# Computing the next head pair's queries and gates inside the attention of the current one

## The chip, the cores and the metric

The kernel runs on the 8 cores of one Trainium2 chip. Each core has five engines with a queue of their own, which meet only through semaphores: TensorE (PE, matmuls; PEld is its weight load), VectorE (DVE), ScalarE (ACT), GpSimd (POOL) and SyncE (SP, which only issues DMAs). An engine runs its own instructions in the order in which the program wrote them. The metric is the time of the slowest core in microseconds, median over runs; lower is better.

## The reference

One encoder layer, applied to one sequence of 8192 tokens ("p") and four of 2048 ("s"), width 2048. There are 8 heads of kind A (global attention, two key/value heads) and 8 of kind B (a neighbourhood of 8 by 16 positions plus a learned bias); both see 16 meta tokens ahead of the sequence.

```python
u = rms_norm(h, norm_w) @ w_in
qa, ka, va, za, qb, kb, vb, zb = split(u)
qa = rope(rms_norm(qa, q_norm_a)); ka = rope(rms_norm(ka, k_norm_a))
ya = softmax(qa @ ka.T * scale) @ va * silu(za)             # all tokens
qb = rms_norm(qb, q_norm_b); kb = rms_norm(kb, k_norm_b)
yb = softmax(qb @ kb.T * scale + bias, window + meta) @ vb * silu(zb)
y  = h + concat(ya, yb) @ w_out
```

## The kernel before, in words

No core talks to another. Each does four chunks of 512 query tokens: two of the long sequence (64 key tiles, `nt = 64`, chunks 0 and 1), then two of a short one (`nt = 16`, chunks 2 and 3). Keys and values of the A heads are computed once for a sequence and stay in SBUF (`KAT`, `VAE`).

**A chunk.** Nine tiles of 128 tokens are normalised and transposed into `xnTl`. Then four *head pairs* `hp` = 0 to 3 are done, each with two B heads and two A heads, and last the output projection. Of the six groups of 256 weight columns that a pair needs, four are for B (`qb`, `kb`, `vb`, `zb`), two for A: `qa` (queries) and `za` (gates, through Silu). A *projection* is 16 matmuls of 128x256 into one PSUM buffer (`proj`, L331). `qb` has 4 of them, `kb` 9, `vb` 9, `zb` 4, `qa` 4, `za` 4. The work of each pair:

- `gen_bproj(hp)`: the B projections. It begins with the bias tiles `BT`, four times two DMAs on the POOL queue (L545), then a POOL add of the mask (L548), all one behind the other. It is a generator; each `next` does one *step*: one projection, and for `qb` and `kb` also the statistics of the item before (ACT L352 to L357, POOL L361) and the last part of the item before that (`qk_final`: DVE L392, two transposes L397, copies L404). With the steps that only drain, B has 6 + 11 + 9 + 4 = 30 steps.
- `battn(hp)`: B attention, 8 items (L594 to L625), exponentials on ACT (L607 to L611). It is the reader of `BT`.
- `aphase(hp)`: first `qa` with rope (POOL L368, L376 and L382 beside L361; 4 items in 6 steps), then `za` (4 steps). Then, for each of two heads, A attention in *units* of two key tiles: scores `S` (L666, two matmuls of 128x512), one exponential over 128x1024 (L671), and `PV` (L693, 8 matmuls). That is 33 units a head for `nt = 64` and 9 for `nt = 16`, the last of each with only the 16 meta tokens. While they run, a step of `gen_bproj(hp + 1)` is called after every second unit (`nt = 64`) or after each (`nt = 16`).

**Buffers.** Outside A attention a projection takes turns between two PSUM buffers in `psA`. During A attention, `S` uses `psA`, and all projections share one buffer in `ps_m` ("single" mode): the next can start only when the last has been copied out. What is left of the generator after attention (12 steps for `nt = 16`, none for `nt = 64`) runs with two buffers again. The A queries `QTA` and gates `ZGA` exist once.

**Weights.** Two slots `ws`. `nextw()` hands out a group and issues the load of the one behind it. In chunk 0 that is a DMA on the POOL queue with a cast (L253), a multiplication of 4.4 us on DVE (L255), and a store to DRAM on SP; afterwards it is one DMA on SP. The rope tables of `qa` come through SP too (L411).

**The activation table.** Silu needs another table on ACT than Exp, Ln and Square do. Each change shows as an ACT_TABLE_LOAD in front of the instruction.

## Time and profile before

| | |
|---|---|
| median of 2 runs | 4385.31 us (4384.64 to 4385.98) |
| the profiled execution | 4396.51 us |
| its span, from the first instruction to the last | 4395.5 us (core 2, the slowest) |
| spans of the eight cores | 4344.3 to 4395.5 us |
| busy PE / PEld / ACT / DVE / POOL | 66 / 50 / 43 / 26 / 22% of the span |
| mean granted TensorE clock | 0.845 of full speed |
| ACT_TABLE_LOAD | 1283 ns each; 40 in front of L671, 34 of L523, 16 of L526 |

The span is the sum of stages with different limits, so its averages say little. The page was read for the sizes of things, the table of stretches for the stages, and the list in order of time for what each stage waits for. Full clock is 2.4 GHz; a granted share of 0.50 is 1.2 GHz.

### The profile page before, as it was taken

The numbers are of one execution on the slowest core, as the hardware profiler recorded it, in microseconds if no ns is written. First come the engines' busy times: TensorE is split into PE (matmuls) and PEld (weight loads), VectorE is DVE, ScalarE is ACT, GpSimd is POOL, SyncE is SP. The second block draws the span as 40 slices with busy tenths as digits, with TensorE's granted clock in tenths as the row PEclk, the third lists the DMA queues.
The fourth block names the chain that finished last, engine by engine and source line by source line (L and its number), as shares of the span: only waits on it lengthen the run. The fifth ranks groups of instructions, "written<-read, shape, count | busy, mean of one in ns | idle before, by whom it ended". The sixth has DMA issues, their size and how long they took to land.

```text
span 4395.5 us, 74263 instructions; the slowest of 8 cores (4344.3 to 4395.5 us)
## 1 busy us (share of the span) xinstructions
PE 2906.0 (66%) x24964; PEld 2191.3 (50%) x24964; DVE 1138.5 (26%) x2810; ACT 1902.1 (43%) x4001; POOL 959.1 (22%) x1463
## 2 busy tenths in 40 slices
PE   3777465758566734777776776666676766677677
PEld 2666343535444423554554545554554555455455
DVE  4666432222222002211111102522122113222221
ACT  3777423635444603354545561643343304333330
POOL 2555413030211001211112100513213200321310
PEclk9999687979887966988878898988888877788788
DMA  5555745242422267211112005632313352322214
GB/s 146 195 195 195 152 80 72 49 65 49 78 45 51 44 133 164 61 35 48 28 37 39 34 31 194 180 102 44 64 44 54 58 163 105 55 60 47 44 56 132
DMA packets 331472, 376.61 MB, mean 86 GB/s; under 512 B 177504, under 2 KB 299104, under 8 KB 299104
## 3 DMA queue, kind: packets, MB, share of 16 engines
q1 hardware_dynamic: 76176, 298.36, 19.8%
q0 software_dynamic: 236496, 56.72, 14.5%
q10 hardware_dynamic: 18432, 16.79, 1.1%
q8 instruction: 212, 3.47, 0.3%
q14 instruction: 156, 1.28, 0.1%
HBM read 376.09 MB, written 52.43 MB: 97 GB/s over the span
## 4 chain that ended last, share of the span: by engine, by line
PE 46%; DMA 18%; ACT 13%; issue 9%; DVE 7%; POOL 6%; ACTq 0%; DVEq 0%; SPq 0%; POOLq 0%
PE psA L331 21%; PE ps_m L331 10%; DMA BT<-rw 8%; ACT PT L671 6%; PE ps_o L693 5%; PE psA L666 4%; DMA xres<-xloc 3%; POOL BT L548 2%; DVE qtok L392 2%; DMA xf<-xloc 2%; PE psA L319 2%; DMA ws<-w_out 2%; PE ps_m L397 2%; DMA ws<-w_in 1%; POOL BT L545 1%
## 5 line engine op out<-in xcount | busy, mean ns | idle before, releaser
L331 PE MATMUL psA<-ws,xnTl 128*128 128x256 bf16 x7488 | 970.7, 295 | 13.5 <-DVE VBE L519 6.2
L671 ACT ACTIVATE PT<-psA,negc 128x1024 bf16<-128x1024 f32 x640 | 685.7, 1111 | 627.7 <-PE psA L666 625.9
L331 PEld LDWEIGHTS psA<-ws,xnTl 128*128 128x128 bf16 x7488 | 780.0, 106 | 156.4 <-issue 16.7
L361 POOL TENSOR_TENSOR wxg<-wk,gt 128x256 f32<-128x256 f32 x354 | 259.0, 733 | 2096.9 <-DVE wk L346 2082.9
L693 PEld LDWEIGHTS ps_o<-VAE,PT 128*128 128x128 bf16 (+1 forms) x5248 | 341.9, 100 | 483.1 <-issue 434.2
L693 PE MATMUL ps_o<-VAE,PT 128*128 128x129 bf16 (+1 forms) x5248 | 427.6, 226 | 229.3 <-ACT PT L671 223.8
L331 PE MATMUL ps_m<-ws,xnTl 128*128 128x256 bf16 x3840 | 518.5, 294 | 38.7 <-DVE wk L346 38.7
L397 PE MATMUL ps_m<-identb,qtok 128*128 128x128 bf16 x708 | 103.3, 230 | 632.7 <-DVE qtok L392 632.5
L304 ACT ACTIVATE xb<-xf 128x2048 bf16<-128x2048 f32 x118 | 225.4, 1910 | 524.3 <-DMA xf<-xloc 352.8
L331 PEld LDWEIGHTS ps_m<-ws,xnTl 128*128 128x128 bf16 x3840 | 392.5, 105 | 106.8 <-issue 40.4
L666 PE MATMUL psA<-QTA,KAT 128*128 128x512 bf16 x1280 | 405.3, 405 | 10.9 <-ACT ZGA L526 10.9
L352 ACT ACTIVATE wt<-wk 128x128 f32<-128x128 f32 x708 | 218.3, 308 | 432.8 <-DVE wk L346 387.6
L331 PE MATMUL psA<-ws,OT 128*128 128x256 bf16 x2048 | 284.4, 310 | 173.5 <-DVE ysb L735 170.7
L397 PEld LDWEIGHTS ps_m<-identb,qtok 128*128 128x128 bf16 x708 | 49.3, 99 | 693.8 <-issue 693.8
L331 PEld LDWEIGHTS psA<-ws,OT 128*128 128x128 bf16 x2048 | 224.3, 111 | 233.1 <-issue 182.8
L319 PE MATMUL psA<-identb,xb 128*128 128x128 bf16 x1888 | 157.6, 250 | 228.9 <-DVE xb L310 227.9
L319 PEld LDWEIGHTS psA<-identb,xb 128*128 128x128 bf16 x1888 | 136.9, 113 | 246.4 <-issue 238.6
L548 POOL TENSOR_TENSOR BT<-BT,cmb 128x1280 bf16<-128x1280 bf16 x64 | 171.7, 2683 | 400.2 <-DMA BT<-rw 392.9
L419 DVE RECIPROCAL rl<-ps_o 128x1 f32<-128x1 f32 x256 | 41.9, 164 | 686.0 <-PE ps_o L693 431.3
L376 POOL TENSOR_TENSOR wt<-wxg,rope 128x64 f32<-128x64 f32 x584 | 169.3, 322 | 174.5 <-ACT wt L352 174.5
L310 DVE TENSOR_SCALAR xb<-xf,st 128x2048 bf16<-128x2048 f32 x118 | 155.1, 1315 | 170.4 <-ACT st L308 170.1
L523 ACT ACT_TABLE_LOAD x34 | 43.6, 1283 | 293.9 <-PE psA L331 239.6
(74 smaller groups left out, 2989.6 us busy)
## 6 DMA issues: line engine op xcount, KB each, us to landing
ws<-wbf SPq DMA_DIRECT2D x98, 1024.0 KB, 5.1
xf<-xall_p SPq DMA_DIRECT2D x64, 1024.0 KB, 5.3
xf<-xloc SPq DMA_DIRECT2D x38, 1024.0 KB, 6.6
wbf<-ws SPq DMA_DIRECT2D x34, 1024.0 KB, 4.6
ws<-w_in POOLq DMA_DIRECT2D x26, 1024.0 KB, 9.2
BT<-rw POOLq DMA_DIRECT2D x128, 160.0 KB, 5.2
xres<-xloc SPq DMA_DIRECT2D x128, 128.0 KB, 4.7
y<-ysb ACTq DMA_DIRECT2D x128, 128.0 KB, 3.5
```

The lines of the kernel that those rows point to most:

```text
L304: op("act", lambda: ACTE.activation(out=xb[i][:], in_=xf[i][:], func=ACT.Square, accum_out=st[i][:, 0:1]), reads=[t_xf[i]], writes=[t_xb[i ...
L310: op("dve", lambda: DVE.tensor_scalar(out=xb[i][:], in0=xf[i][:], scalar1=st[i][:, 2:3], scalar2=None, op0=ALU.mult), reads=[t_xf[i], t_st ...
L319: op("pe", lambda c=c, hf=hf, c8=c8: PE.transpose(out=pst(hf)[:, c8, :], in_=xb[i][:, c * 128:(c + 1) * 128], identity=identb[:]), reads=[ ...
L331: op("pe", lambda c=c: PE.matmul(psu(pu), lhsT=xT_fn(c), rhs=ws[wslot][:, c, :], start=(c == 0), stop=(c == 15)), reads=txl + [t_ws[wslot] ...
L352: op("act", lambda h=h: ACTE.activation(out=wt2[k][:, h * 128:(h + 1) * 128], in_=wk[k][:, h * 128:(h + 1) * 128], func=ACT.Square, accum_ ...
L361: op("pool", lambda: POOL.tensor_tensor(out=v3(wxg[k]), in0=v3(wk[k]), in1=gb, op=ALU.mult), reads=[t_wk[k], t_gt], writes=[t_wxg[k]])
L376: op("pool", lambda hh=hh, s_=s_: POOL.tensor_tensor(out=ov[:, 2 * hh:2 * hh + 2, s_, :], in0=xv[:, 2 * hh:2 * hh + 2, 1 - s_, :], in1=sv[ ...
L397: op("pe", lambda h=h: PE.transpose(out=ps_m[:, m, h * 128:(h + 1) * 128], in_=qtok[q_][:, h * 128:(h + 1) * 128], identity=identb[:]), re ...
L548: op("pool", lambda bi=bi: POOL.tensor_tensor(out=BT[bi][:].rearrange("p h (r c) -> p (h r) c", r=10), in0=BT[bi][:].rearrange("p h (r c) ...
L666: op("pe", lambda c=c, bank=bank: PE.matmul(psA[:, bank, :], lhsT=KAT[:, g, c * 128:(c + 1) * 128], rhs=QTA[:, hl, :], start=True, stop=True),
L671: op("act", lambda: ACTE.activation(out=PT[p_][:].rearrange("p (a n) -> p a n", a=2), in_=psA[:, 2 * sp_:2 * sp_ + 2, :], func=ACT.Exp, bi ...
L693: op("pe", lambda j=j, c=c, i_=i_, kc=kc: PE.matmul(pso(j), lhsT=PT[p_][:kc, i_ * 512 + j * 128:i_ * 512 + (j + 1) * 128], rhs=VAE[:kc, c, ...
```

## The change

`QTA` and `ZGA` become pairs of buffers, indexed by `hp % 2`. The `qa` and `za` projections leave `aphase` and become a generator `gen_aproj(hp)`, which `gen_next(hp)` runs behind `gen_bproj(hp)`: 40 steps in all. `gen_next(0)` runs ahead of `battn(0)`, and `gen_next(hp + 1)` is stepped during the A attention of `hp`. The pace is no longer one step for so many units: after unit `u`, as many steps have been called as 46 times `u` over the number of units (66 or 18), rounded down. All 40 are then done after 58 of 66 units, and after 16 of 18. To make room in SBUF, the residual and output tiles `xres` and `ysb` of the output projection now share the buffers of `wxg` and `wt1`.

```diff
@@ -166,14 +166,14 @@
-        QTA = sb("QTA", [128, 2, 512], BF16); t_QTA = Tk()
-        ZGA = sb("ZGA", [128, 4, 256], BF16); t_ZGA = Tk()
+        QTAs = [sb(f"QTA{i}", [128, 2, 512], BF16) for i in range(2)]; t_QTAs = [Tk(), Tk()]
+        ZGAs = [sb(f"ZGA{i}", [128, 4, 256], BF16) for i in range(2)]; t_ZGAs = [Tk(), Tk()]
...
-        xres = [sb(f"xres{i}", [128, 256], F32) for i in range(2)]; t_xres = [Tk(), Tk()]
-        ysb = [sb(f"ysb{i}", [128, 256], F32) for i in range(2)]; t_ysb = [Tk(), Tk()]
+        xres, t_xres = wxg, t_wxg
+        ysb, t_ysb = wt1, t_wt1
@@ -523,8 +523,8 @@
-                            op("act", lambda: ACTE.activation(out=ZGA[:, it["j"], :], in_=psu(pu), func=ACT.Silu),
-                               reads=[t_pu(pu)], writes=[t_ZGA])
+                            op("act", lambda: ACTE.activation(out=it["zga"][:, it["j"], :], in_=psu(pu), func=ACT.Silu),
+                               reads=[t_pu(pu)], writes=[it["t_zga"]])
@@ -638,20 +638,30 @@
-                    def aphase(hp, genB, kstep):
-                        g = hp // 2
+                    def gen_aproj(hp):
+                        QTA, t_QTA, ZGA, t_ZGA = QTAs[hp % 2], t_QTAs[hp % 2], ZGAs[hp % 2], t_ZGAs[hp % 2]
                         wq_ = nextw()
                         items = []
                         for j in range(4):
                             items.append({"kind": "qa", "lt": 2 + j, "j": j, "w": wq_, "gidx": 0, "t_dst": t_QTA,
                                           "dst_fn": (lambda h, j=j: QTA[:, h, j * 128:(j + 1) * 128])})
-                        run_pipe(items, [(2, ip_final), (0, ip_proj), (1, ip_stats)])
+                        yield from gen_pipe(items, [(2, ip_final), (0, ip_proj), (1, ip_stats)])
                         wz_ = nextw()
-                        items = [{"kind": "za", "lt": 2 + j, "j": j, "w": wz_} for j in range(4)]
-                        run_pipe(items, [(0, ip_proj)])
+                        items = [{"kind": "za", "lt": 2 + j, "j": j, "w": wz_, "zga": ZGA, "t_zga": t_ZGA} for j in range(4)]
+                        yield from gen_pipe(items, [(0, ip_proj)])
+
+                    def gen_next(hp):
+                        yield from gen_bproj(hp)
+                        yield from gen_aproj(hp)
+
+                    def aphase(hp, genB, nsteps):
+                        g = hp // 2
+                        QTA, t_QTA, ZGA, t_ZGA = QTAs[hp % 2], t_QTAs[hp % 2], ZGAs[hp % 2], t_ZGAs[hp % 2]
                         if genB is not None:
                             state["pu_mode"] = "single"
                         ucount = [0]
+                        done_steps = [0]
+                        nunits_tot = 2 * (nt // 2 + 1)
@@ -705,19 +715,22 @@
-                                if genB is not None and ucount[0] % kstep == 0:
-                                    next(genB, None)
+                                if genB is not None:
+                                    want = (ucount[0] * nsteps) // nunits_tot
+                                    while done_steps[0] < want:
+                                        next(genB, None)
+                                        done_steps[0] += 1
...
-                    for _ in gen_bproj(0):
+                    for _ in gen_next(0):
                         pass
                     for hp in range(4):
                         battn(hp)
-                        genB = gen_bproj(hp + 1) if hp < 3 else None
-                        aphase(hp, genB, 2 if nt > 16 else 1)
+                        genB = gen_next(hp + 1) if hp < 3 else None
+                        aphase(hp, genB, 46)
```

How it moves instructions, at three places. In these listings, `x16` behind a row counts matmuls, and 16 of L331 are one projection.

**TensorE, chunk 2 (`nt = 16`), from the end of B attention into the first units of A attention.** Before:

```order
L625 MATMUL ps_o<-VBE,PT 128x129
L428 MATMUL ps_m<-identb,og 128x128 x2
L331 MATMUL psA<-ws,xnTl 128x256 x32
L397 MATMUL ps_m<-identb,qtok 128x128 x2
L331 MATMUL psA<-ws,xnTl 128x256 x16
L397 MATMUL ps_m<-identb,qtok 128x128 x2
L331 MATMUL psA<-ws,xnTl 128x256 x16
L397 MATMUL ps_m<-identb,qtok 128x128 x4
L331 MATMUL psA<-ws,xnTl 128x256 x64
L666 MATMUL psA<-QTA,KAT 128x512 x4
L693 MATMUL ps_o<-VAE,PT 128x129 x8
L331 MATMUL ps_m<-ws,xnTl 128x256 x16
```

And now:

```order
L625 MATMUL ps_o<-VBE,PT 128x129
L428 MATMUL ps_m<-identb,og 128x128 x2
L676 MATMUL psA<-QTA,KAT 128x512 x4
L703 MATMUL ps_o<-VAE,PT 128x129 x8
L331 MATMUL ps_m<-ws,xnTl 128x256 x32
L676 MATMUL psA<-QTA,KAT 128x512 x2
L703 MATMUL ps_o<-VAE,PT 128x129 x8
L397 MATMUL ps_m<-identb,qtok 128x128 x2
L331 MATMUL ps_m<-ws,xnTl 128x256 x16
L397 MATMUL ps_m<-identb,qtok 128x128 x2
L331 MATMUL ps_m<-ws,xnTl 128x256 x16
```

The eight A projections are gone from between the two attentions, and two or three steps now follow each unit, into the one buffer `ps_m`. L666 and L693 are L676 and L703 now.

**GpSimd, chunk 0, the bias tiles of the next pair** (a piece of the difference, each row with what it waits for):

```order
 L253 DMA ws<-w_in 128x16x256 [waits d_wst1,pe]
-L545 DMA BT<-rw 64x20x64 x2
-L548 TENSOR_TENSOR BT<-BT,cmb 128x1280 [waits d_bt0]
-L545 DMA BT<-rw 64x20x64 x2
-L548 TENSOR_TENSOR BT<-BT,cmb 128x1280 [waits d_bt1]
-L545 DMA BT<-rw 64x20x64 x2
-L548 TENSOR_TENSOR BT<-BT,cmb 128x1280 [waits d_bt2]
-L545 DMA BT<-rw 64x20x64 x2
+L545 DMA BT<-rw 64x20x64 [waits pe]
+L545 DMA BT<-rw 64x20x64
+L548 TENSOR_TENSOR BT<-BT,cmb 128x1280 [waits d_bt0]
+L545 DMA BT<-rw 64x20x64 [waits pe]
```

Before, the statistics of this pair's `qa` stood in this queue ahead of the bias tiles, and the weight load waited for a TensorE event later than any reader of `BT`. Now those statistics stand one A attention earlier, and each bias tile waits for its own reader in `battn`.

**ScalarE, chunk 0 (`nt = 64`), the gates `za`.** Before:

```order
L352 ACTIVATE wt,wst<-wk 128x128 x2
L355 ACTIVATE wst<-wst,epst 128x2
L357 ACTIVATE wst<-wst 128x2
L526 ACTIVATE ZGA<-psA 128x256 x4
L671 ACTIVATE PT<-psA,negc 128x1024 x5
```

And now:

```order
L526 ACTIVATE ZGA<-ps_m 128x256
L681 ACTIVATE PT<-psA,negc 128x1024
L526 ACTIVATE ZGA<-ps_m 128x256
L681 ACTIVATE PT<-psA,negc 128x1024
L526 ACTIVATE ZGA<-ps_m 128x256
L681 ACTIVATE PT<-psA,negc 128x1024 x2
L526 ACTIVATE ZGA<-ps_m 128x256
L681 ACTIVATE PT<-psA,negc 128x1024 x6
```

Four Silus in a row have become four with exponentials between them. Over the whole program the places where the ACT queue changes between Silu and the other functions go from 101 to 161.

## Rows read from the trace of the kernel before

**Rows 1.** Table of stretches, core 2; columns: stretch, length, each engine's busy time (instructions), clock, DMA share, GB/s
```profile
2032.30:2049.40 17.10, 14.73 (x144) 10.81 (x143) 4.65 (x21) 10.95 (x24) 0.00 (x0) 0.77 0.01 2
2049.40:2083.00 33.60, 22.16 (x138) 15.89 (x137) 6.25 (x20) 8.03 (x29) 17.18 (x31) 0.75 0.30 50
2049.40:2113.40 64.00, 32.23 (x234) 22.96 (x233) 7.89 (x23) 19.17 (x49) 31.94 (x42) 0.75 0.46 58
895.80:980.60 84.80, 34.90 (x233) 24.63 (x234) 21.35 (x26) 19.39 (x49) 34.96 (x44) 0.71 0.57 84
3133.60:3193.40 59.80, 29.29 (x203) 21.52 (x204) 8.34 (x23) 16.04 (x46) 31.90 (x42) 0.75 0.47 62
3193.40:3272.60 79.20, 66.22 (x557) 51.48 (x557) 23.72 (x82) 30.42 (x85) 8.16 (x11) 0.91 0.12 41
```

**Rows 2.** Timeline of PE; columns: start, length, engine, line, operation, count, [idle before, releaser]
```profile
2113.32 0.37 PE L397 MATMUL ps_m<-identb,qtok 128*128 128x128 bf16 x2 [17.08 <-DVE qtok L392]
...
3193.36 0.37 PE L397 MATMUL ps_m<-identb,qtok 128*128 128x128 bf16 x2 [17.17 <-DVE qtok L392]
```

**Rows 3.** Timeline of POOL, the first bias DMAs of a pair, chunk 1 and chunk 2
```profile
2071.79 1.82 POOL L545 DMA_DIRECT2D BT<-rw  x2
...
3154.54 1.82 POOL L545 DMA_DIRECT2D BT<-rw  x2
```

**Rows 4.** Timeline of ACT, A attention without steps (chunk 1, last pair)
```profile
2561.96 2.12 ACT L671 ACTIVATE PT<-psA,negc 128x1024 bf16<-128x1024 f32 x2 [0.34 <-PE psA L666]
2564.42 2.12 ACT L671 ACTIVATE PT<-psA,negc 128x1024 bf16<-128x1024 f32 x2 [0.34 <-PE psA L666]
```

**Rows 5.** Timeline of PE, two `kb` steps with two units between them
```profile
783.07 1.91 PE L331 MATMUL ps_m<-ws,xnTl 128*128 128x256 bf16 x16
...
787.33 1.91 PE L331 MATMUL ps_m<-ws,xnTl 128*128 128x256 bf16 x16
```

**Rows 6.** Timeline of PE, chunk 2: steps with one unit between; then the drain with two buffers
```profile
3205.18 1.91 PE L331 MATMUL ps_m<-ws,xnTl 128*128 128x256 bf16 x16
...
3207.79 1.91 PE L331 MATMUL ps_m<-ws,xnTl 128*128 128x256 bf16 x16
...
3227.91 1.91 PE L331 MATMUL ps_m<-ws,xnTl 128*128 128x256 bf16 x16
...
3231.06 1.91 PE L331 MATMUL ps_m<-ws,xnTl 128*128 128x256 bf16 x16
...
3249.12 18.96 PE L331 MATMUL psA<-ws,xnTl 128*128 128x256 bf16 x160
```

**Rows 7.** Timeline of PE and ACT, a `zb` step with two units before the next
```profile
1994.03 1.91 PE L331 MATMUL ps_m<-ws,xnTl 128*128 128x256 bf16 x16
1996.02 1.28 ACT L523 ACT_TABLE_LOAD   x1 [1.58 <-PE ps_m L331]
1997.31 0.38 ACT L523 ACTIVATE ZG<-ps_m 128x256 bf16<-128x256 f32 x1
1997.71 1.28 ACT L671 ACT_TABLE_LOAD   x1
1999.01 2.12 ACT L671 ACTIVATE PT<-psA,negc 128x1024 bf16<-128x1024 f32 x2
2000.71 1.91 PE L331 MATMUL ps_m<-ws,xnTl 128*128 128x256 bf16 x16
...
2016.33 3.53 PE L331 MATMUL ps_m<-ws,xnTl 128*128 128x256 bf16 x16
2024.69 0.59 PE L666 MATMUL psA<-QTA,KAT 128*128 128x512 bf16 x2
```

**Rows 8.** Timeline of PE, the first `qa` projections and the last `qa` transposes between the attentions
```profile
2050.65 5.16 PE L331 MATMUL psA<-ws,xnTl 128*128 128x256 bf16 x32
...
2072.70 0.37 PE L397 MATMUL ps_m<-identb,qtok 128*128 128x128 bf16 x2 [3.80 <-DVE qtok L392]
```

**Rows 9.** Waits by who waited for whom: total us, times, longest
```profile
DVE ws L255 <- DMA ws<-w_in: 137.0, 17, 13.7
```

## The prediction

> **What bounds the kernel now.** I read three views, in this order. The page first: no engine is busy for more than 66% of the span, so the time lies in waits and in the order of things, and a total over an engine decides nothing. The table of stretches second, cut where TensorE changes its work, since the change touches only what lies between one B attention and the next; there are 12 such stretches (three for each of four chunks). Then the list in order of time inside one stretch of each kind.
>
> A B attention lasts 17.1 us and POOL does nothing in it. Behind it come 33.6 us of `qa` and `za` projections, in which TensorE is busy for 22.2 [rows 1]. POOL's bias tiles begin only when the `qa` statistics have left its queue, at 2071.79 [rows 3]. TensorE then gets a little into A attention and stands for 17 us before the first transposes of the next pair's `qb` [rows 2], because POOL's part of `qb` is queued behind four bias tiles. The chain from the first bias DMA to those transposes takes 2113.32 − 2071.79 = 41.5 us in chunk 1, and 3193.36 − 3154.54 = 38.8 us in chunk 2 [rows 2, 3]. So each stretch has a first part, from the end of B attention to those transposes: 64.0 us in chunk 1, 84.8 in chunk 0 (there a cast weight load stands in POOL's queue and waits for `za`), 59.8 in chunks 2 and 3 [rows 1]. The rest is projections threaded through A attention.
>
> **The first part.** In the new order POOL's queue holds nothing between the previous A attention and the bias tiles, and the first tile is free when the second of eight score blocks of B attention has read it, about 3 us into 17.1 (an estimate: the blocks follow each other evenly). The chain is then 14.1 us along when B attention ends, and the transposes come 41.5 − 14.1 = 27.4 us behind its end for `nt = 64`, 24.7 for `nt = 16`. TensorE has reached them by then: it has five units and two projections to do (one unit for `nt = 16`), some 12 us. It still waits, but less. The first part saves 64.0 − 27.4 = 36.6 us in chunk 1, 84.8 − 27.4 = 57.4 in chunk 0, 59.8 − 24.7 = 35.1 in chunks 2 and 3. The eight projections are of course not gone; they come back below. The chain may be some us shorter beside an idle SP queue or longer beside B attention; I take it as it is.
>
> **The rest, `nt = 64`.** A unit alone costs 2.46 / 2 = 1.23 us and ACT sets it [rows 4]. A `kb` step with two units takes 4.26 [rows 5], so the step itself costs 1.8; with one unit it is 3.15 − 1.23 = 1.9 [rows 6]. TensorE is what they cost. Four `qa` steps at 1.9 and two draining ones at about 0.6 make 9 us. Rope makes POOL's part longer: the four items took 22.05 us in all where nothing was beside them [rows 8], that is up to 5.5 each, against a pace of 1.43 units a step, 3.6 us. So the lower bound is 9 and the upper 22 − 11 for the nine units that run meanwhile, which is 11. I keep 9.
>
> `za` is dearer. A Silu step with two units took 6.68 us at full clock: table load 1.28, Silu 0.38, load 1.28, exponential 1.06, and TensorE waits for all of it [rows 7]. Four of them took 2024.69 − 1994.03 = 30.7, since the clock fell to 1.2 GHz in the later ones (a projection of 3.53 instead of 1.91). In the new order two of four have one unit between, which costs ACT's own 1.28 + 0.38 + 1.28 + 1.06 = 4.0, and two have two: 2 × 4.0 + 2 × 6.7 + 2 for the clock = 23.5 us for six units, so 16 us net. The same denser pace takes `zb` from 30.7 − 8 × 1.23 = 21 to 16, a gain of 5. With one unit less ahead of the transposes (+1.2) and small change for `kb` and `vb` (−1), the rest grows by 9 + 16 − 5 = 20 us. Between the listed places, 60 table loads more in the queue are 77 us of ACT, most of it inside these terms.
>
> Here the Trainium skill speaks against the change. ScalarE: Activation LUTs, section What ACT_TABLE_LOAD costs, gives about 2.66 us for every switch, a load of 1283 ns and a drain of about 1380. By that 60 more switches would cost another 83 us. The load agrees with the trace, the drain does not: the exponential's load starts 0.02 us behind the Silu's end and the exponential 0.02 us behind the load [rows 7].
>
> Chunk 1: −36.6 + 20.5 = −16 a stretch, **−48** for three.
>
> **Chunk 0** also loads its weights with a DVE multiplication behind a wait of up to 13.7 us [rows 9], and DVE holds the copy that frees the one projection buffer. Before, `za`'s weights landed during B attention. Now the load is issued behind the last `zb`; about 10 us of DMA and 4.4 of multiplication pass, and the first rope table waits behind the store on SP: about 15 us of standing at `qa` (an estimate from these durations), 7 at `vb` (whose cover, two draining steps, shrinks from four units to three), 2 elsewhere. Bounds: nothing, if units fill it, and 3 × 18 = 54 (three waits of 13.7 and 4.4). I take 24: −57.4 + 20.5 + 24 = −13 a stretch, **−39** for three.
>
> **The rest, `nt = 16`.** 40 steps on 18 units. Here steps bound, not ACT: a `kb` step takes 3.15 us with a unit inside [rows 6], since TensorE waits for copy and `qtok` on DVE, and a unit fits in that gap for nothing. What the short sequence did with two buffers cost 1.9 us a projection (18.96 for ten [rows 6]). In one buffer it must wait for the copy: 2.62 with a unit inside [rows 6], about 2.5 without. Eight `vb`: +5. Four `zb` with two table changes: 12.7 against 7.6, +5. `qa`: POOL's chain again, 22.05 before [rows 8], about 21 now, and units hide in it. `za`: 12.7. Sum +44 on 79.2 [rows 1], so −35 + 44 = +9 a stretch, **+52** for six. Between bounds: +30 (zb and za at 1.9 each, as with two buffers) and +55 (each Silu step at the 4.0 of ACT and `qa` at 22).
>
> **At nothing:** the A projections of pair 0 still run with two buffers, only ahead of its B attention, and the last pair has no stretch behind it: its lost gap and the first's kept one cancel. `xres` and `ysb` in other tiles: the readers of these are an A attention earlier.
>
> **Sum:** −48 − 39 + 52 = −35 us on the profiled 4396.51 us, and that run lies 11.2 above the median of the runs shown. Forecast 4385.3 − 35 = **4350 us**, −0.8%.
>
> **Rivals.**
> - *The waits of chunk 0 are covered and the short chunks break even*: −72 and −52 more, −159, 4226 us. For it: in chunk 0 the part behind the first transposes now has three such loads and hardly shows them; units can fill. Against: `za`'s weights lose the whole of B attention as cover. Half of it already gives 4290. Chance 0.24.
> - *Silu costs more*: TensorE idles 3 us in each such step and all go at 1.2 GHz. From rows 7 the last took 2024.69 − 2016.33 = 8.4 instead of 6.7; 1.7 on eight steps and six stretches is +82, so 4432 us. The drain that the Trainium skill names (ScalarE: Activation LUTs, same section) would give +83, by itself. For the mechanism: the clock did fall there. Against: one-unit steps idle less. Chance 0.15.
> - *Slower than before*: the bias chain does not start inside B attention, because something in POOL's queue still waits for its end. Then the 14.1 us come back twelve times, +169, 4519 us. From 3 us of delay a stretch on it is no gain, from 10 us it is over 2%. Against: before, the tiles were fetched as soon as POOL was free, 11 us ahead of A attention [rows 1, 3], and each now waits for its own reader. Chance 0.08.
> - That projections remain outside the attention is excluded by the order.
>
> **Numbers.** The forecast keeps 0.53. A measurement of this kernel tells about 2% (88 us) from no change: 4298 and 4473. Faster by over 2%: most of the first rival and a little of the forecast's lower end, 0.25. Slower: the third and a part of the second, 0.09. Within: 0.66. The bounds of the weights (−72, +90) and of the short chunks (−84, +66) are independent; by the root of their squares they give −111 and +112, 4239 to 4462. With the rivals added, 4250 to 4430 leaves out 2 in 10.
>
> **What would show it.** Bias DMAs that start about 3 us into B attention, and first transposes 25 to 28 us behind its end; if they come at 40, the third rival. A wait of TensorE for 12 to 15 us there still. Silu steps at 4 and 6.7 us, and 161 table loads of 1283 ns with nothing between them. In chunk 0, a stand of some 15 us at the first `qa` step. Stretches shorter by some 16 us in chunk 1, and of about 148 us in chunks 2 and 3 (before: 59.8 + 79.2 = 139.0 [rows 1]). The prediction is wrong if the short chunks' stretches shrink, or if chunk 0's grow.

## The result, and the profile after

The change does not make the kernel faster. Its median is 4433.24 us (21 runs, 4406.35 to 4559.51), that of the kernel before 4415.68 us (20 runs beside it); the ratio of the runs compared is **1.0069 [1.0049, 1.0089]**, 0.7% slower. The forecast was 4350 us, range 4250 to 4430, 0.8% faster: wrong in sign. The profiled execution took 4423.45 us. Of the profiled executions the mean span of the eight cores is compared from here on, 4374.0 us before and 4395.1 after, since the cores of one execution spread over some 50 us and which is slowest changes. Some executions of both kernels ran in a slower state; the medians hold them, the ratio and every mean span below leave them out, and without them the changed kernel's median is 4420.2 us.

A mean span has a spread of its own. The changed kernel's lay between 4390 and 4412 us in fourteen executions (mean 4398.8), that of the kernel before between 4348 and 4391 in thirteen beside the experiments (mean 4362). The pair that is taken apart below thus shows 21 us of a loss that is rather 30 (by the ratio) or 37 (by these means), and a difference of under some 15 us between two mean spans is not told from none.

The page of the changed kernel, part 1:

```profile
span 4422.4 us, 74136 instructions; the slowest of 8 cores (4374.5 to 4422.4 us)
...
PE 2931.4 (66%) x24964; PEld 2197.8 (50%) x24964; DVE 1151.8 (26%) x2810; ACT 1989.4 (45%) x4061; POOL 962.8 (22%) x1463
```

The averages hardly moved, and again decide nothing. The table of stretches does. This one was cut as before, for every core at the end of a B attention and the start of the next, and averaged over the eight cores (us):

| part of the span | before | after | difference | predicted |
|---|---|---|---|---|
| up to the first B attention | 630.7 | 679.1 | +48.4 | cancels with the last pairs |
| chunk 0, three stretches | 695.1 | 669.8 | −25.3 | −39 |
| chunk 1, three stretches | 604.6 | 569.8 | −34.8 | −48 |
| chunks 2 and 3, six stretches | 839.7 | 921.6 | +81.9 | +52 |
| behind the B attention of the last pairs, four | 1321.7 | 1277.8 | −43.9 | cancels |
| 16 B attentions | 282.2 | 276.9 | −5.3 | 0 |
| **sum** | 4374.0 | 4395.1 | **+21.1** | −35 |

The same stretches on core 1 after the change, first part and whole; they answer to [rows 1] (chunk 0, chunk 1, chunk 2; columns as there):

```profile
953.00:974.80 21.80, 10.42 (x88) 7.12 (x88) 7.71 (x8) 8.84 (x18) 12.60 (x9) 0.77 0.60 78
953.00:1171.10 218.10, 144.10 (x1239) 103.33 (x1239) 58.75 (x110) 114.15 (x192) 40.66 (x54) 0.87 0.35 64
2065.40:2090.10 24.70, 10.28 (x86) 7.21 (x87) 2.52 (x7) 8.84 (x18) 12.62 (x9) 0.74 0.54 34
2065.40:2256.60 191.20, 139.40 (x1239) 101.84 (x1239) 32.38 (x104) 113.91 (x192) 34.03 (x48) 0.91 0.17 41
3138.30:3161.40 23.10, 9.19 (x57) 5.88 (x57) 2.51 (x7) 5.72 (x15) 12.65 (x9) 0.66 0.52 33
3138.30:3295.90 157.60, 101.44 (x759) 73.40 (x759) 31.96 (x104) 53.76 (x136) 34.06 (x48) 0.83 0.21 49
```

The first parts have shrunk from 85, 64 and 60 us to 22, 25 and 23. What was gained there has been given back behind them.

**The bias chain.** POOL around the B attention that ends at 2065.38 (chunk 1), then TensorE's first transposes behind it; they answer to [rows 2, 3]:

```profile
2051.69 1.81 POOL L545 DMA_DIRECT2D BT<-rw  x2 [41.30 <-PE psA L601]
2058.90 2.60 POOL L548 TENSOR_TENSOR BT<-BT,cmb 128x1280 bf16<-128x1280 bf16 x1 [5.40 <-DMA BT<-rw]
2061.45 1.79 POOL L545 DMA_DIRECT2D BT<-rw  x2
2068.36 2.60 POOL L548 TENSOR_TENSOR BT<-BT,cmb 128x1280 bf16<-128x1280 bf16 x1 [5.12 <-DMA BT<-rw]
```

```profile
2077.13 0.61 PE L703 MATMUL ps_o<-VAE,PT 128*128 128x129 bf16 x8 [0.47 <-ACT PT L681]
2090.11 0.37 PE L397 MATMUL ps_m<-identb,qtok 128*128 128x128 bf16 x2 [12.37 <-DVE qtok L392]
```

The first DMA is issued 13.7 us before B attention ends, the chain to the transposes takes 38.4 us, and TensorE still stands for 12.4 of them. Each add waits about 5 us for its own DMA: DMA and add are one behind the other, four times.

**A Silu among exponentials.** ACT during the four `zb` steps of that stretch, then TensorE at the second of them and the granted clock there; they answer to [rows 7]:

```profile
2177.95 1.28 ACT L523 ACT_TABLE_LOAD   x1 [1.04 <-PE ps_m L331]
2179.24 0.38 ACT L523 ACTIVATE ZG<-ps_m 128x256 bf16<-128x256 f32 x1
2179.64 1.28 ACT L681 ACT_TABLE_LOAD   x1
2180.94 2.12 ACT L681 ACTIVATE PT<-psA,negc 128x1024 bf16<-128x1024 f32 x2
2185.86 1.28 ACT L523 ACT_TABLE_LOAD   x1 [2.81 <-PE ps_m L331]
...
2189.98 1.28 ACT L523 ACT_TABLE_LOAD   x1
...
2197.98 1.28 ACT L523 ACT_TABLE_LOAD   x1 [2.89 <-PE ps_m L331]
```

```profile
2182.20 0.61 PE L703 MATMUL ps_o<-VAE,PT 128*128 128x129 bf16 x8 [3.01 <-ACT PT L681]
2182.65 3.08 PE L331 MATMUL ps_m<-ws,xnTl 128*128 128x256 bf16 x16
```

```profile
2182.00:2185.50 3.50, 3.30 (x24) 2.62 (x25) 0.00 (x0) 1.06 (x2) 0.00 (x0) 0.67 0.00 0
```

From load to load it is 7.9, 4.1 and 8.0 us: 4.1 with one unit between, 8.0 with two. In the steps with two, TensorE stood for 3.0 us and its next projection then took 3.08 and 2.80 us at a lower clock instead of 1.91. That is not new: the same distance averages 7.3 us in the long stretches of the kernel before, and after the change 7.55 at `zb` and 8.35 at `za`. 161 loads of 1283 ns stand in the trace, as counted.

**`qa` in one buffer.** TensorE in that stretch (the bracket gives the time for which it stood), then the first and the last of POOL's instructions for the four items:

```profile
2207.46 0.27 PE L397 MATMUL ps_m<-identb,qtok 128*128 128x128 bf16 x2 [0.47 <-DVE qtok L392]
...
2211.43 0.27 PE L397 MATMUL ps_m<-identb,qtok 128*128 128x128 bf16 x2 [1.05 <-DVE qtok L392]
...
2219.90 0.27 PE L397 MATMUL ps_m<-identb,qtok 128*128 128x128 bf16 x2 [3.03 <-DVE qtok L392]
```

```profile
2202.45 0.73 POOL L361 TENSOR_TENSOR wxg<-wk,gt 128x256 f32<-128x256 f32 x1 [66.34 <-DVE wk L346]
...
2218.33 0.72 POOL L382 TENSOR_TENSOR wt<-wt 128x256 f32<-128x256 f32 x1
```

POOL needs 16.6 us for the four items, with gaps of 1.2 us at most inside them. Ahead of them stand the first projection and its copy (2.65 us from 2199.80 on), behind them the last transposes and two units before `za` (2222.77).

**A short stretch.** TensorE in chunk 2: `vb` steps at the end of the first head, then the last `za` steps:

```profile
3213.43 0.40 PE L703 MATMUL ps_o<-VAE,PT 16*128 16x129 bf16 x4
3214.25 1.91 PE L331 MATMUL ps_m<-ws,xnTl 128*128 128x256 bf16 x16 [0.42 <-DVE VBE L519]
3216.90 1.91 PE L331 MATMUL ps_m<-ws,xnTl 128*128 128x256 bf16 x16 [0.75 <-DVE VBE L519]
3219.55 1.91 PE L331 MATMUL ps_m<-ws,xnTl 128*128 128x256 bf16 x16 [0.75 <-DVE VBE L519]
3222.73 0.22 PE L428 MATMUL ps_m<-identb,og 128*128 128x128 bf16 x1 [1.27 <-DVE rl L419]
...
3228.20 3.33 PE L331 MATMUL ps_m<-ws,xnTl 128*128 128x256 bf16 x16
...
3273.68 3.58 PE L331 MATMUL ps_m<-ws,xnTl 128*128 128x256 bf16 x16
3279.16 3.42 PE L331 MATMUL ps_m<-ws,xnTl 128*128 128x256 bf16 x16 [1.90 <-ACT ZGA L526]
...
3287.37 1.91 PE L331 MATMUL ps_m<-ws,xnTl 128*128 128x256 bf16 x16 [2.16 <-ACT ZGA L526]
...
3292.22 0.38 PE L703 MATMUL ps_o<-VAE,PT 16*128 16x129 bf16 x4 [2.06 <-ACT PT L690]
3293.47 0.27 PE L428 MATMUL ps_m<-identb,og 128*128 128x128 bf16 x1 [0.88 <-DVE rl L419]
```

`vb` steps follow each other at 2.65 us, waiting for DVE's copy out of the one buffer, where two buffers took 1.9 a projection [rows 6]. Behind the last `za` the attention's own end stands uncovered. In the kernel before, twelve steps were left for it and the time after it.

### The profile page after: what moved, and what is told of

The parts are those of the page before. It is cut to its first block, busy times and chain, and to the rows that moved or that the text cites. A ratio compares the mean times of both kernels' runs of the same rounds, so it can differ in the third digit from the quotient of the medians.

```text
span 4422.4 us, 74136 instructions; the slowest of 8 cores (4374.5 to 4422.4 us)
## 1 busy us (share of the span) xinstructions
PE 2931.4 (66%) x24964; PEld 2197.8 (50%) x24964; DVE 1151.8 (26%) x2810; ACT 1989.4 (45%) x4061; POOL 962.8 (22%) x1463
## 3 DMA queue, kind: packets, MB, share of 16 engines
q0 software_dynamic: 236496, 56.72, 14.3%
## 4 chain that ended last, share of the span: by engine, by line
PE 45%; DMA 19%; ACT 12%; issue 10%; DVE 7%; POOL 6%; DVEq 0%; ACTq 0%; SPq 0%; POOLq 0%
PE ps_m L331 16%; PE psA L331 15%; DMA BT<-rw 6%; ACT PT L681 6%; PE ps_o L703 4%; PE psA L676 4%; DMA ws<-w_in 3%; DMA wxg<-xloc 3%; DVE qtok L392 3%; POOL BT L548 2%; DMA xf<-xloc 2%; PE psA L319 2%; PE ps_m L397 2%; DMA ws<-w_out 2%; ACT L681 1%
## 5 line engine op out<-in xcount | busy, mean ns | idle before, releaser
L681 ACT ACTIVATE PT<-psA,negc 128x1024 bf16<-128x1024 f32 x640 | 694.6, 1111 | 721.6 <-PE psA L676 713.7
L331 PE MATMUL ps_m<-ws,xnTl 128*128 128x256 bf16 x6528 | 895.1, 297 | 178.5 <-DVE wk L346 56.9
L331 PEld LDWEIGHTS ps_m<-ws,xnTl 128*128 128x128 bf16 x6528 | 670.7, 106 | 325.4 <-issue 205.5
L331 PE MATMUL psA<-ws,xnTl 128*128 128x256 bf16 x4800 | 589.5, 285 | 23.3 <-DVE ws L255 13.7
L703 PEld LDWEIGHTS ps_o<-VAE,PT 128*128 128x128 bf16 (+1 forms) x5248 | 356.5, 103 | 439.6 <-issue 386.0
L703 PE MATMUL ps_o<-VAE,PT 128*128 128x129 bf16 (+1 forms) x5248 | 441.3, 230 | 180.9 <-ACT PT L681 163.8
L331 PEld LDWEIGHTS psA<-ws,xnTl 128*128 128x128 bf16 x4800 | 483.5, 102 | 96.3 <-issue 25.0
L676 PE MATMUL psA<-QTA,KAT 128*128 128x512 bf16 x1280 | 424.6, 422 | 0.0
L331 PE MATMUL psA<-ws,OT 128*128 128x256 bf16 x2048 | 282.0, 309 | 162.4 <-DVE wt L748 159.8
L331 PEld LDWEIGHTS psA<-ws,OT 128*128 128x128 bf16 x2048 | 224.0, 111 | 220.1 <-issue 171.2
L346 DVE COPY wk<-ps_m 128x256 f32<-128x256 f32 x204 | 86.6, 425 | 523.9 <-PE ps_m L331 521.3
```

The lines of the kernel that those rows point to most:

```text
L331: op("pe", lambda c=c: PE.matmul(psu(pu), lhsT=xT_fn(c), rhs=ws[wslot][:, c, :], start=(c == 0), stop=(c == 15)), reads=txl + [t_ws[wslot] ...
L676: op("pe", lambda c=c, bank=bank: PE.matmul(psA[:, bank, :], lhsT=KAT[:, g, c * 128:(c + 1) * 128], rhs=QTA[:, hl, :], start=True, stop=True),
L681: op("act", lambda: ACTE.activation(out=PT[p_][:].rearrange("p (a n) -> p a n", a=2), in_=psA[:, 2 * sp_:2 * sp_ + 2, :], func=ACT.Exp, bi ...
L703: op("pe", lambda j=j, c=c, i_=i_, kc=kc: PE.matmul(pso(j), lhsT=PT[p_][:kc, i_ * 512 + j * 128:i_ * 512 + (j + 1) * 128], rhs=VAE[:kc, c, ...
```

## The experiments

Two theories stood after the comparison. **The gain is the bias chain's**, begun inside B attention, and would come without moving a projection; the move itself gives nothing and costs it back where steps crowd (chunks 2 and 3) and at Silus. The rival: **the projections inside A attention are the gain**, as their 33.6 us between the attentions suggest. Where a comparison of timed runs gave no ratio, the mean span of the profiled execution is used.

Mean over cores, us; "first" is the first part of one stretch, the next columns whole sets of stretches:

| kernel | mean span | first: chunk 0, 1, 2 and 3 | chunk 0 (3) | chunk 1 (3) | chunks 2, 3 (6) |
|---|---|---|---|---|---|
| before | 4374.0 | 86.9, 62.0, 59.9 | 695.1 | 604.6 | 839.7 |
| after | 4395.1 | 26.0, 22.7, 21.8 | 669.8 | 569.8 | 921.6 |
| after, bias late | 4591.3 | 45.9, 36.6, 37.5 | 724.1 | 610.4 | 1018.7 |
| after, long chunks only | 4324.1 | 24.1, 21.2, 58.9 | 661.6 | 566.9 | 838.6 |
| after, 18 steps in short chunks | 4261.5 | 24.7, 21.9, 20.9 | 664.6 | 566.1 | 799.5 |
| after, no Silu table | 4230.7 | 26.9, 22.3, 22.1 | 623.5 | 512.1 | 877.1 |
| after, bias DMAs together | 4290.3 | 25.2, 12.9, 12.0 | 659.4 | 537.4 | 850.2 |
| after, no rope in `qa` | 4296.9 | 24.8, 21.5, 21.2 | 652.2 | 555.2 | 864.7 |
| before, bias early | 4188.0 | 75.6, 49.0, 44.9 | 654.3 | 559.2 | 737.6 |
| before, bias early, gates by Exp, 1/x | 4342.9 | 88.5, 55.4, 51.7 | 697.9 | 546.5 | 810.2 |
| before, bias early, gates by Exp, Ln | 4279.5 | 84.1, 51.7, 48.3 | 699.4 | 554.4 | 769.6 |
| after, 18 steps, bias together | 4179.3 | 24.8, 13.0, 12.0 | 659.7 | 538.3 | 737.2 |
| the same, gates by Exp, Ln | 4185.5 | 23.8, 13.1, 12.0 | 679.9 | 499.3 | 744.0 |
| after, 18 steps, bias together, gates by Exp, 1/x | 4256.3 | 24.4, 12.9, 12.1 | 675.6 | 495.9 | 791.0 |

**1. The bias chain held back until B attention has ended** (changed kernel).

```diff
 def gen_bproj(hp):
+    if hp > 0: wait("pool", state["bend"])    # TensorE's last event of battn
```

> The changed kernel, with one wait more: POOL may fetch the bias tiles of the next pair only when B attention has ended. Theory (the early start of the bias chain is what pays for this change): the chain starts about 14 us later in each of 12 stretches, so the first qb transposes come 36 to 40 us behind the end of B attention instead of 22 to 26, and the kernel gets about 12 x 14 = 170 us slower than the changed one, 1.04 to 1.05 of the kernel before. Rival (the first part is bound by TensorE's own work or the weights, and the bias tiles merely lie beside it): within 1% of the changed kernel, 1.00 to 1.015.

Ratio 1.0553 [1.0528, 1.0579] to the kernel before. POOL's first bias DMA in the second stretch of chunk 1, where B attention ended at 2121.48, and the transposes:

```profile
2123.33 1.80 POOL L547 DMA_DIRECT2D BT<-rw  x2 [56.83 <-PE psA L678]
...
2157.82 0.37 PE L397 MATMUL ps_m<-identb,qtok 128*128 128x128 bf16 x2 [24.00 <-DVE qtok L392]
```

The wait doubles from 12.4 to 24.0 us, and the twelve stretches grow by 192 us (54.3 + 40.6 + 97.1). Without the early chain the change costs 5.5%.

**2. A projections moved in the long chunks only.**

```diff
-    yield from gen_aproj(hp)
+    if nt > 16: yield from gen_aproj(hp)      # else: run whole, behind the attention
...
-    aphase(hp, genB, 46)
+    aphase(hp, genB, 46 if nt > 16 else 18)
```

> The change only for the two chunks of the long sequence; the two short chunks run as before (A projections between the attentions, one step a unit). Theory (costs are local to a stretch, and the short chunks alone make the change a loss): the six short stretches go from 153.6 back to 140 us, so 82 us less than the changed kernel, ratio about 0.988. Rival (what the change costs lies in the long chunks or in shared places such as the first chunk's start): the ratio stays at 1.00 or above.

Ratio 0.9889 [0.9835, 0.9942]; the short chunks are back at 838.6, and the long ones keep their gain. The loss is the short chunks' alone.

**3. In the short chunks one step for each unit again, the rest behind attention with two buffers.**

```diff
-    aphase(hp, genB, 46)
+    aphase(hp, genB, 46 if nt > 16 else 18)
```

> The changed kernel with one step a unit in the short chunks: 18 of the 40 steps run under attention, 22 behind it with two PSUM buffers and the Silus of a group in a row. Theory (too many steps through one buffer, with Silu between exponentials, is what the short chunks pay for): a short stretch takes 22 us to the first transposes, 80 for what it did before and some 31 for qa and za, 133 instead of 153.6, so 124 us less than the changed kernel, ratio about 0.98. Rival (POOL's and DVE's chains bound 40 steps wherever they stand): stretches of 150 us and more, ratio 1.00 to 1.01.

A short stretch takes 133.3 us, not 153.6, and the mean span is 2.6% under the 4374.0 of before (2.3% under the mean of its eight executions beside this run). On core 1 one of them is this:

```profile
3106.07:3238.70 132.63, 98.60 (x759) 74.17 (x759) 31.50 (x105) 46.63 (x131) 33.66 (x48) 0.82 0.20 49
```

PE's busy time is 98.6 here and 101.4 in the changed kernel's row above, the length 25 us less: nearly all that went were waits.

**4. Copy in place of Silu, no table changes** (the gates' nonlinearity is left out).

```diff
-    ACTE.activation(out=ZG[:, it["j"], :], in_=psu(pu), func=ACT.Silu)
+    ACTE.activation(out=ZG[:, it["j"], :], in_=psu(pu), func=ACT.Copy)   # za likewise
```

> The changed kernel with Copy in place of Silu: the gates are left without their nonlinearity, all else the same. ACT then needs no second table. Theory (table changes between exponentials are dear because TensorE stands for them): Silu steps fall to the price of a vb step, 2.6 or 4.2 us, about 20 us less in a long stretch and 8 to 10 in a short one, 170 us in all, ratio about 0.967. Rival (the loads only cost their own 1.28 us where ACT is the bound, and the fall of the clock has other causes): at most 161 loads x 1.28 = 206 us less busy ACT but under 80 us of time, ratio 0.99.

A stretch of chunk 1 is 19.2 us shorter, one of chunk 0 15.4, a short one 7.4. Table changes are dearest where ACT sets the pace. The mean span falls by 164 us.

**5. The eight bias DMAs issued together, behind `battn`, the four adds where they were.** In the changed kernel, then, as the strongest test of the rival, in the kernel before, which moves no projection:

```diff
+    def bias_dma(hp): ...                     # the 8 DMAs, taken out of gen_bproj
 battn(hp)
+if hp < 3: bias_dma(hp + 1)
```

> The changed kernel, with all eight bias DMAs of the next pair put into POOL's queue right behind B attention's code, and the four mask additions behind them, instead of DMA and addition by turns. Theory (the first part is bound by the serial bias chain): the DMAs land during B attention, the additions take 4 x 2.6 us, and TensorE meets its transposes when it has done five units and two projections, 12 to 14 us behind B attention instead of 22 to 26; some 9 us less in each of 12 stretches, 110 us, ratio about 0.98. Rival (the first part is bound by the DMA engines or the weights): the first part stays over 20 us and the ratio at 1.00 to 1.01.

> The kernel before (A projections still between the attentions), with the bias DMAs put right behind B attention's code, ahead of the qa statistics in POOL's queue, and the mask additions left where the generator starts. Theory (what the change wins is the bias chain's early start, and that needs no moved projection): the first part falls from 62 to 47 us in chunk 1, from 87 to about 65 in chunk 0, from 60 to 41 in the short chunks, 225 us in all, ratio about 0.95. Rival (moving the projections is what opens the way, since POOL's queue or TensorE's 33 us of projections hold the rest): less than 60 us, ratio over 0.985.

The first gives 105 us of mean span, the second **186 us** (4374.0 to 4188.0, 4.3%; against the two executions of the kernel before beside it, 4356 and 4369, it is 4.0%). POOL in that second kernel, a stretch of chunk 1 whose B attention ends at 1987.99:

```profile
1974.52 1.81 POOL L544 DMA_DIRECT2D BT<-rw  x2 [86.54 <-PE psA L604]
1979.70 1.76 POOL L544 DMA_DIRECT2D BT<-rw  x2 [3.37 <-PE ps_m L428]
1982.77 1.76 POOL L544 DMA_DIRECT2D BT<-rw  x2 [1.30 <-PE psA L604]
1986.09 1.76 POOL L544 DMA_DIRECT2D BT<-rw  x2 [1.55 <-PE psA L604]
...
2010.30 10.46 POOL L551 TENSOR_TENSOR BT<-BT,cmb 128x1280 bf16<-128x1280 bf16 x4
```

The tiles arrive under B attention, and the four adds cost their own 10.5 us behind the `qa` statistics. TensorE reaches the transposes without a wait, 49 us behind the end, and eight projections lie inside these 49. The edit does two things, it starts the DMAs sooner and takes the adds from between them; in the old order the two are not told apart. Either way the rival is refuted: one edit of where DMAs are issued, in the old order, does more than the whole change.

In chunk 0 the batch does not shorten the first part (25.2 after 26.0). Something else holds it there, on core 6 in the stretch whose B attention ends at 943.65. DVE, then TensorE:

```profile
956.64 4.42 DVE L255 TENSOR_TENSOR ws<-ws,normw 128x4096 bf16<-128x4096 bf16 x1 [11.29 <-DMA ws<-w_in]
```

```profile
961.55 3.57 PE L331 MATMUL ps_m<-ws,xnTl 128*128 128x256 bf16 x16 [9.76 <-DVE wk L346]
```

The second projection waits 9.8 us for a copy that stands in DVE's queue behind the multiplication of the next weights. There the recorded rival of this experiment, the weights, holds.

**6. Both together, and the short pace.** The best of the changed order:

> The changed kernel with one step a unit in the short chunks and early, batched bias DMAs; Silu stays. Set beside the kernel before with the same early bias DMAs (4188 us mean span), it prices the moved A projections alone. Theory (nearly all that the move won was the bias chain's early start): short stretches of 122 us against 123, long ones of 179 and 220 against 186 and 218, mean span about 4174, within 0.5% of that version; ratio to the kernel before about 0.955. Rival (the move is worth its own 33 us gap): 2% or more below that version, 0.935.

Ratio 0.9564 [0.9455, 0.9672], mean span 4179.3. Against the old order with early bias it is 8.7 us better, 0.2%: +47.6 up to the first B attention, −37.6 behind the last pairs, −20.9 in chunk 1, +5.4 in chunk 0, −0.4 in the short chunks, −2.7 in the B attentions. Three executions of this kernel have mean spans of 4168 to 4179, three of the other, on another chip, 4176 to 4188: what moving the projections is worth on its own cannot be told from nothing. Both kernels beat the two of the comparison. The first transposes in a stretch whose B attention ends at 2043.78 no longer wait:

```profile
2043.63 10.28 POOL L551 TENSOR_TENSOR BT<-BT,cmb 128x1280 bf16<-128x1280 bf16 x4
```

```profile
2057.86 0.28 PE L397 MATMUL ps_m<-identb,qtok 128*128 128x128 bf16 x2
```

**7. Gates without the Silu table**, with the exponential's. First as z / (1 + exp(−z)), with DVE's reciprocal, in the changed and the old order:

```diff
+    DVE.tensor_copy(out=wk[k][:], in_=psu(pu))
+    ACTE.activation(out=wt2[k][:], in_=wk[k][:], func=ACT.Exp, scale=-1.0)
+    DVE.tensor_scalar(... scalar1=1.0, op0=ALU.add)
+    DVE.reciprocal(out=wt2[k][:], in_=wt2[k][:])
+    DVE.tensor_tensor(out=dst, in0=wk[k][:], in1=wt2[k][:], op=ALU.mult)
```

> The changed kernel with three edits: one step a unit in the short chunks, bias DMAs batched and early, and the gates computed as z / (1 + exp(-z)) with Exp on ACT and four DVE operations, so that ACT needs no second table. Theory (the costs found are independent): 4262 us mean span with the pace alone, less 110 for the bias DMAs, less about 115 for the gates in the long chunks, 4040 us, ratio about 0.92. Rival (the four DVE operations hold the one projection buffer's copies up, or the clock falls as more work is packed): 0.95 and above.

> The kernel before with early bias DMAs and with the gates through Exp and DVE, the A projections still between the attentions. Theory (with the bias chain out of the way, moving qa and za under the long attention is worth little: it saves 33 us of gap and costs some 20 once Silu is cheap; in the short chunks it is worth nothing): 225 us less for the bias, about 50 less for the gates of zb, 4100 us mean span, ratio about 0.94, that is 1 to 2% above the version with the moved projections. Rival (the move pays as soon as its two costs are gone): 4% or more above that version.

4256.3 and 4342.9, the old order 2.0% above the changed one: both theories failed in the time that they gave. One reason is DVE's row of the costliest groups of the second kernel:

```profile
L517 DVE RECIPROCAL wt<-wt 128x256 f32<-128x256 f32 x128 | 224.4, 1753 | 13.2
```

Then as z · exp(−ln(1 + exp(−z))), three functions of ACT, with a copy and one product on DVE:

> The kernel before with early bias DMAs and the gates as z x exp(-ln(1 + exp(-z))): three short ACT functions of the table that is loaded anyway, a DVE copy ahead of them and one DVE product behind. Theory (what failed in the gates through a DVE reciprocal was the reciprocal of 1.75 us and the buffer behind it, not the idea): zb in a long stretch falls by about 10 us, nothing changes in a short one, mean span 4188 - 6 x 10 = 4125, ratio about 0.943. Rival (each gate's chain over two engines holds the buffers whatever the functions): 4188 or more, 0.957 and above.

> The changed kernel with one step a unit in the short chunks, early, batched bias DMAs and the same three-function gates. Theory (costs add): 4174 less about 17 us in each of six long stretches, mean span about 4070, ratio 0.93, the fastest of all. Rival (as for the other kernel with these gates): 4174 or more, 0.955.

Ratios 0.9779 [0.9678, 0.9879] and 0.9591 [0.9545, 0.9636]; the rival held both times. Without the reciprocal the mean spans are 63 and 71 us shorter, so it was part of the cost. In the changed order chunk 1 gains 39 us of the sum (538.3 to 499.3; experiment 4 gained 57.7), but the time up to the first B attention (+20.5) and chunk 0 (+20.2), where DVE has the weights to multiply too, lose as much. That DVE is their cause is argued from its rows in the old order, not shown. In the old order it is 91 us worse than with Silu, 54 of them in the twelve first parts. Its rows show that the copy and the product join DVE's queue, that TensorE waits for the copy, and DVE for ACT's third function:

```profile
L333 PE MATMUL psA<-ws,xnTl 128*128 128x256 bf16 x7488 | 976.5, 296 | 54.3 <-DVE wk L514 40.6
...
L521 DVE TENSOR_TENSOR ZGA<-wk,wt 128x256 bf16<-128x256 f32 x64 | 68.9, 1077 | 114.7 <-ACT wt L519 114.7
```

The mean of 1077 ns hides something: the same product takes 426 in the changed order. DVE and POOL on core 0 of the old order:

```profile
727.48 9.40 DVE L521 TENSOR_TENSOR ZGA<-wk,wt 128x256 bf16<-128x256 f32 x1 [1.72 <-ACT wt L519]
```

```profile
726.32 10.27 POOL L564 TENSOR_TENSOR BT<-BT,cmb 128x1280 bf16<-128x1280 bf16 x4
```

Between the attentions the `za` products meet POOL's mask additions, which start earlier now that the bias tiles have landed. All 14 of the 64 that began beside an addition lasted until 0.3 us behind the end of one, 1.3 to 9.4 us in all; the other 50 took 0.43. In the changed order the gates lie elsewhere and none is held. How much of the 91 us this makes, no run tells.

**8. `qa` without rope on POOL** (the queries are not rotated).

```diff
-    if r is not None:
+    if r is not None and item.get("kind") != "qa":
```

> The changed kernel with the six POOL instructions of rope left out for each qa item (the table is still loaded; the queries are not rotated, so that part of the computation is missing). Theory: POOL's chain of weight product and rope sets the pace of the qa steps, where the prediction had the TensorE step of 1.9 us: in chunk 1 the qa part of a stretch falls from 23.1 us to about 20 (8.9 units at 1.23 and 9 for the steps), in chunks 2 and 3 from 21.1 to about 15, in chunk 0 by no more than in chunk 1. Three stretches of 3, three of 3 or less and six of 6 make about 54 us, and the four pairs 0, where qa stands alone, some 10 each: mean span 4395 to about 4300. Rival: the one projection buffer and its copy set the pace, POOL hides: each qa part changes by under 1 us, and only the pairs 0 give something, mean span 4355 or more.

The `qa` part falls from 23.1 to 19.7 us in chunk 1, from 21.1 to 14.0 in the short chunks and from 37.4 to 31.7 in chunk 0 (by 5.7, more than was expected), the mean span to 4296.9. POOL's chain sets the pace of `qa`, and this is the term of the prediction with the largest error in a long stretch.

## Why the prediction was wrong, step by step

In short: the step that failed is the price of steps threaded through A attention in one buffer, "+20.5" a long stretch and "+44" a short one; the runs show +27.7 and +51.7. The saving that it was set against was right.

**What bounds the kernel**: right. The bias chain behind `qa`'s statistics was the wait that ended last, and experiments 1 and 5 show it from both sides (+196 and −186 us).

**The first part**: right, and a little low. Forecast 27.4, 27.4 and 24.7 us behind the end of B attention in chunk 0, in chunk 1 and in the short chunks; measured 26.0, 22.7 and 21.8. The head start was 13.7 us for an estimate of 14.1; the chain takes 38.4 instead of 41.5 us, and 36.1 instead of 38.8 in chunk 2, which the text had named as possible. With the means of eight cores this saves 60.9, 39.3 and 38.1 where 57.4, 36.6 and 35.1 stood: 37 us more gain in all than forecast. In chunk 0 the nearness is partly luck: with the bias chain out of the way (experiment 5) the first part there is still 25.2 us, by a wait for the weights that the forecast of 27.4 did not hold.

**The rest** failed, by 7 to 8 us in every one of the twelve stretches: 92 us. Less those 37, this is but for rounding the 56 us between −35 and +21. By groups of steps (means of eight cores; in the long chunks each unit is taken at 1.23 us):

| term | predicted | measured |
|---|---|---|
| long: `qb`, `kb`, `vb` | −1 | +1.0 |
| long: `zb` and `za` with the attention's end | +11 | +13.5 |
| long: `qa` | +9 | +12.0 |
| long: one unit less ahead of the transposes | +1.2 | +1.2 |
| **long, sum** | +20.5 (its terms give 20.2) | +27.7 |
| chunk 0 on top | +24 | +24.8 |
| short: `qb`, `kb` | 0 | −7.0 |
| short: `vb` | +5 | +9.7 |
| short: `zb` | +5 | +6.1 |
| short: `qa` | +21 | +21.1 |
| short: `za` to the next B attention | +12.7 | +21.7 |
| **short, sum** | +44 | +51.7 |

- *`qa` at 9 us.* The prediction had bounds of 9 and 11 and kept the lower, TensorE's. It should have kept the other: POOL's items with rope pace these steps. The measured 12.0 lies even above the upper bound, since the first projection with its copy and the last transposes stand outside POOL's 16.6 us. Experiment 8 takes the rope away and gets 19.7 − 9 × 1.23 = 8.6, near the 9 of the forecast. Two buffers are no cure: in experiment 3 `qa` runs with two in the short chunks and takes 23.1 us, with one 21.1.
- *Silu.* A step with one unit between costs ACT's own 4.1, as forecast. With two it is 6.7 to 9.1 in the kernel before and 6.7 to 8.8 in the changed one, by the clock at which the next projection runs; the 6.7 of [rows 7] is the case of full clock. The four `zb` steps of a long stretch take 22.9 us, where 23.5 stood. What was missed lies in `za`, whose last projection takes 3.2 us on average, while the last of the threaded steps before, a `zb`, took 2.1. The rival "Silu costs more" had this mechanism, the clock, and asked for 82 us; over the long stretches it gave 2.5 each, 15 in all. The drain that would have given 83 us is not in the trace either: each load ends 0.01 to 0.02 us before what follows.
- *Short chunks.* Two places had no term, the ends of the two heads' attention, put at nothing without a reason. When 40 steps share 18 units, the ends of both heads (TensorE waits for DVE's `rl`, 3219.55 to 3228.20 above) stand among single-buffer steps, and the second end stands behind everything. Before, the end of attention was followed by the twelve steps of the drain. Part of this is only moved: `qb` and `kb` are 7.0 us shorter, while `vb` has 4.7 and `za` 9.0 more than forecast. Experiment 3 puts the drain back: `za` to the next B attention falls from 21.7 to 10.1 us, `zb` from 14.3 to 7.3, `vb` from 31.6 to 21.9, while `kb` is again 38.0 and `qa` 23.1.
- *Chunk 0's weights*: right, 24.8 for 24 (2.8 at `kb`, 8.0 at `vb`, 14.3 at `qa`). The predicted stand of some 15 us at the first `qa` step is DVE's wait for the weights, which holds the copy out of the one buffer; on core 1 the second `qa` projection starts at 1115.34, 13.2 us after the first:

```profile
1110.44 4.42 DVE L255 TENSOR_TENSOR ws<-ws,normw 128x4096 bf16<-128x4096 bf16 x1 [16.41 <-DMA ws<-w_in]
```

- *At nothing*: the first start costs 48.4 and the last pairs give back 43.9, with a smaller B attention (−5.3) a sum of −0.8. Right, though the start differs by up to 18 us between kernels that share its code (678.5 in experiment 3, 696.3 in experiment 2), for a reason that no run settled.

**The rivals.** Covered waits in chunk 0 (0.24) did not come; a bias chain that is not early (0.08) did not either, but experiment 1 made it: 4619.6 us where 4519 was worked out. The price per microsecond was right: on core 1 the chain then began 1.9 us behind the end of B attention instead of 13.7 ahead of it, 15.6 us later, and a stretch got 16.0 us longer. Of the 101 us between 4519 and 4620, 70 are the base: 4420 instead of 4350. The true outcome had no rival of its own, because nearly every term of the rest erred to the same side, by one to nine microseconds, and the bounds were combined by the root of their squares as if independent. Not all of them are: `vb`, `zb` and `za` share the wait for a single projection buffer that something other than TensorE must free. That this is why they erred together is argued, not shown; `qa` erred by POOL's own time.

## What to carry to other kernels

When a change both moves work and lets a chain start earlier, price them apart and try the early start alone: here DMAs issued one phase sooner gave 4% by themselves, and the move of eight projections nothing that can be told on top. A step that is threaded through other work in one buffer costs what frees that buffer (a copy, a table change) or what its chain needs on another engine (POOL's rope), not what TensorE needs for it; take that upper bound, and look for the drains that used to cover an end. Errors of terms that share such a cause add up over the number of repeats, so the range must add them too. And before work is put on a second engine, look at what a third does at that moment: gates on DVE were held up by POOL's additions.

## What was not expected of the hardware

- POOL's additions hold some DVE instructions and leave others alone. In the old order with gates by Exp and Ln, core 0, a product of two SBUF tiles (`ZGA<-wk,wt`) takes 0.43 us alone and on average 3.4 us in the 14 cases in which it began beside a `BT` addition, each until 0.3 us behind the end of one; `qtok<-wt,wst` 0.6 alone and 2.7 beside. Copies from PSUM take the same in both cases (`wk<-psA` 0.42, `QTA<-ps_m` 0.22), and so does `ysb<-psA,xres`, which reads one tile of each (0.42).
- DVE's reciprocal of 128x256 f32 takes 1753 ns, where its copy of the same size takes 425 (L346) and a product that nothing holds 425: four times as long. The Trainium skill (VectorE: DVE Perf Modes, section First, the fixed hardware budget) says that it runs as an iterative division repeated eight times; the factor of four is what these runs show.
- ACT's time in the same gate by three table functions is 416 + 507 + 416 ns, 1.34 us, against 1.28 + 0.38 + 1.28 = 2.94 for Silu with both loads. The shorter one lost anyway, through DVE.
- With the bias DMAs issued together, each as its reader lets it, their starts lie 3.1 to 5.2 us apart (1974.52 to 1986.09); with an add behind each, 9.8 us (2051.69, 2061.45), and the adds then take 2.6 us each in either order.
